# Two transformer blocks in one kernel: the same tiles at other places in the on-chip memory

## What is computed

```python
h = h + conformer_conv(h, ...)
h = h + swiglu_ffn(h, ...)
kv = shared_kv(h, ...)
h = h + nsa_attention(h, ..., kv)
h = h + swiglu_ffn(h, ...)
x = rmsnorm(h, final_norm)
for layer in range(2):
    h = rms_norm(x, g_mix[layer])
    x = x + (even_mixer(h, ...) if layer == 0 else odd_mixer(h, ...))
    x = x + memory_cross_attention(rms_norm(x, g_xa[layer]), m, ...)
    x = x + swiglu(rms_norm(x, g_ffn[layer]), ...)
```

## Time and profile before

| what | value |
|---|---|
| median of 3 runs | 2776.31 us (2769.07 to 2776.97) |
| the profiled execution | 2776.31 us, of which the span of its instructions is 2774.5 us |
| mean granted TensorE clock | 0.965 |
| TensorE busy with products | 2632.7 us, 95% of the span |
| VectorE, ScalarE, GpSimd busy | 51%, 34%, 13% |
| DMA | 219.83 MB, 79 GB/s over the span |

### The profile page before, as it was taken

How to read it: one execution, slowest core, us unless ns; L and a number is a source line. 1 busy time by engine, 2 the same in 40 slices (tenths; PEclk the granted TensorE clock), 3 DMA queues, 4 the chain that set the end, 5 groups by cost and what they waited for, 6 DMA issues and landing times.

```text
span 2774.5 us, 34029 instructions
## 1 busy us (share of the span) xinstructions
PE 2632.7 (95%) x12132; PEld 2150.2 (77%) x12132; DVE 1403.0 (51%) x2125; ACT 942.1 (34%) x1645; POOL 350.1 (13%) x312
## 2 busy tenths in 40 slices
PE   6988999999889999999989898999999999899999
PEld 5866888887777788888768686788887877688887
DVE  5885544335577544434443565544433656544422
ACT  4554332222366333322333434323222124332321
POOL 2002000110055400012100040200011050200000
PEclk9999999999699999999998999999999999999999
DMA  4202333233100133323321022233323322133232
GB/s 147 74 1 61 101 96 97 76 108 120 64 1 1 46 99 93 96 76 106 100 84 31 16 82 71 76 97 93 92 84 103 98 90 91 42 102 95 91 101 69
DMA packets 61006, 219.83 MB, mean 79 GB/s; under 512 B 7136, under 2 KB 7392, under 8 KB 60400
## 3 DMA queue, kind: packets, MB, share of 16 engines
q1 hardware_dynamic: 58896, 209.15, 24.2%
q0 software_dynamic: 2016, 9.44, 1.0%
HBM read 216.47 MB, written 2.10 MB: 79 GB/s over the span
## 4 chain that ended last, share of the span: by engine, by line
PE 87%; DVE 8%; ACT 2%; issue 2%; POOL 0%; DMA 0%; DVEq 0%; ACTq 0%; SPq 0%; POOLq 0%
PE psum L212 25%; PE psum L213 25%; PE psum L214 24%; DVE conv_out L847 2%; PE psum L1796 2%; PE psum L1774 1%; DVE wl L195 1%; PE psum L1158 1%; PE psum L1210 1%; ACT wh L189 1%; PE psum L1756 1%; PE psum L1757 1%; PE psum L2581 1%; PE psum L1977 1%; DVE xl L748 1%
## 5 line engine op out<-in xcount | busy, mean ns | idle before, releaser
L212 PE MATMUL psum<-xh,wh 128*128 128x512 f32 x1880 | 744.7, 396 | 51.8 <-DVE xl L748 25.4
L213 PE MATMUL psum<-xl,wh 128*128 128x512 f32 x1880 | 740.0, 394 | 0.0
L214 PE MATMUL psum<-xh,wl 128*128 128x512 f32 x1880 | 739.1, 393 | 0.0
L189 ACT ACTIVATE wh<-raw 128x1024 fp32r<-128x1024 f32 x404 | 421.0, 1055 | 790.2 <-PE psum L214 790.2
L195 DVE TENSOR_TENSOR wl<-raw,wh 128x1024 fp32r<-128x1024 f32 x404 | 532.2, 1330 | 262.5 <-ACT wh L189 261.7
L212 PEld LDWEIGHTS psum<-xh,wh 128*128 128x128 f32 x1880 | 357.0, 190 | 132.5 <-DVE xl L748 31.0
L214 PEld LDWEIGHTS psum<-xh,wl 128*128 128x128 f32 x1880 | 356.9, 190 | 77.0 <-issue 1.5
L213 PEld LDWEIGHTS psum<-xl,wh 128*128 128x128 f32 x1880 | 356.9, 190 | 74.8 <-issue 1.2
L212 PE MATMUL psum<-hidden_high,wh 128*128 128x512 f32 x704 | 276.0, 392 | 0.0
L213 PE MATMUL psum<-hidden_low,wh 128*128 128x512 f32 x704 | 274.1, 389 | 0.0
L214 PE MATMUL psum<-hidden_high,wl 128*128 128x512 f32 x704 | 274.0, 389 | 0.0
(11 more groups left out here) (381 smaller groups left out, 3354.8 us busy)
## 6 DMA issues: line engine op xcount, KB each, us to landing
raw<-ffn_in SPq DMA_DIRECT2D x176, 512.0 KB, 3.5
raw<-ffn_out SPq DMA_DIRECT2D x64, 448.0 KB, 4.1
raw<-ffn_out SPq DMA_DIRECT2D x32, 512.0 KB, 3.6
raw<-pw SPq DMA_DIRECT2D x24, 512.0 KB, 3.6
raw<-o_w_hgg SPq DMA_DIRECT2D x12, 512.0 KB, 4.2
raw<-w_q SPq DMA_DIRECT2D x8, 512.0 KB, 3.6
raw<-w_o SPq DMA_DIRECT2D x8, 512.0 KB, 3.5
raw<-e_w_qk SPq DMA_DIRECT2D x8, 512.0 KB, 3.6
```

The source lines that it names most:

```text
L189: self.nc.scalar.activation(self.wh[:, slot, :], self.raw[:, slot, :], ACT.Copy).then_inc(self.weights_high.sem, 1)
L212: nc.tensor.matmul(out, ah, bh, start=start, stop=False)
L213: nc.tensor.matmul(out, ah, bl, start=False, stop=False)
L214: return nc.tensor.matmul(out, al, bh, start=False, stop=stop)
```

## The change

The order in which `Core.__init__` places its tiles is another one. Sizes, arena offsets, stages, instructions, waits and their order stay as they are.

```diff
-        self.wh = self.place("wh", [P, SLOTS, PANEL], FR)
-        self.wl = self.place("wl", [P, SLOTS, PANEL], FR)
+        self.x = self.place("x", [P, KD, S])
         self.xh_at = self.at
         self.xh = self.place("xh", [P, KD, S], FR)
         self.xl_at = self.at
         self.xl = self.place("xl", [P, KD, S], FR)
-        self.arena0 = self.at
-        self.at += ARENA * 1024
-        self.x = self.place("x", [P, KD, S])
         self.raw = self.place("raw", [P, SLOTS, PANEL])
+        self.wh = self.place("wh", [P, SLOTS, PANEL], FR)
+        self.wl = self.place("wl", [P, SLOTS, PANEL], FR)
         self.rstd = self.place("rstd", [P, S])
...
-        self.ssq_at = self.at
         self.ssq = self.place("ssq", [P, S])
...
         self.eps = self.place("eps", [P, 1])
+        self.arena0 = self.at
+        self.at += ARENA * 1024
         self.psum = ctx.enter_context(nc.psum_tensor("psum", [P, 8, S], F32))
```

## The result

| | before | after |
|---|---|---|
| median, us | 2774.06 (2769.07 to 2777.38, 6 runs) | 2795.11 (2792.77 to 2796.22, 6 runs) |
| ratio, 95% interval | | 1.0077 (1.0063 to 1.009) |
| profiled execution, its span | 2776.31, 2774.5 | 2795.92, 2794.1 |
| mean granted TensorE clock | 0.965 | 0.965 |
| instructions | 34029 | 34029 |

The forecast was 2776 us (2768 to 2782), no change. The kernel is slower by 0.77%, which is where the second rival lay (2792 to 2798).

A forecast was written before the change was run, and what follows sets the result against it. TensorE, busy 95% of the span and 87% of the chain, was taken as the bound. With no instruction changed, every address term was put at 0 us, summing to 0 on the profiled 2776.31: 2776 us, range 2768 to 2782.

The forecast's parts named there:

- the second rival: Arena trains in feed-forward second products and six attention and mixer outputs don't settle: 16 to 22 us slower, 2792 to 2798; chance 0.21.
- Nothing for instructions, order and waits: All queues: no instruction removed, added or moved, no wait goes by an address, loop starts cost the same; 0 us.
- Moves by multiples of 256, 0 us: Tiles outside the arena move by multiples of 256 bytes; the region leaves no mark on the products' pitch; 0 us.
- The arena's new rest on products, 0 us: Large products streaming arena tiles, start at rest 32 in place of 128: constant relation, so trains settle at 226.7 ns again; 0 us.
- a rule by lines of 16 bytes: Skill's rule for SBUF reads: accesses within a 16-byte line run at full rate, so a multiple of 32 is as good as 64.
- The bound of 16.3 to 21.5 us if it doesn't settle: 3264 arena-streaming products at 5.0 ns more each (pitch of `Gates`) or 6.6 ns more (taps' 233.3).
- Nothing hides it: TensorE is the bound where the arena's products run, so a slower pitch there would show in full, 16.3 to 21.5 us.
- The count of 3264: Large products that stream an arena tile: 3 x 704 for `hidden` and 3 x 64 for each of six tiles.
- GpSimd, 0 us: Arena work in the cross-attentions, 8 pairs per layer: taken as 0, with 6 us kept as an end; as a rival, chance 0.05.
- DMA, 0 us: `raw` keeps its rest, SyncE's queue is idle nearly always, loads into the arena come early and are few; 0 us.
- VectorE, 0 us: VectorE's taps read rows at all multiples of 4, median 740 ns, against 744 on even rows; 0 us.

The follow-up runs named there:

- the steps of 32: Kernel of trains alone: weight start moves on 32 bytes from product to product, moving operand with it, eight constant differences; 230.8 to 234.2 ns a product.
- the alternating trains: Kernel of trains alone: products alternate between two pairs of weight and moving starts, own or next weights in step; 232.1 and 230.4 ns with 32, 228.5 and 230.0 with 128.
- the constant trains: Kernel of trains alone, 48 products each at one fixed difference of moving and weight start: 226.7 ns at 0, 229.2 at 64, 233.3 at 32, 234.2 at 160.

## Why the prediction was wrong

- *Nothing for instructions, order and waits*: right. The count is 34029 in both, and the kernel with the same new order and the arena at a rest of 128 takes the time before.
- *Moves by multiples of 256, 0 us*: right, and shown: 928 products of `xh` in the same 210 us, and a ratio of 1.0005 with all other tiles in new places.
- *The arena's new rest on products, 0 us*: this is the step that failed, in the sentence "My reading is that such a train settles at 226.7 again". It took the 226.7 of the earlier trace rows as the pitch of any train with a constant relation, when it was the pitch of one relation, difference 0, which all settled trains of the kernel before happened to have. A train does settle, but at a pitch of its own: 234.2 at 160, 233.1 to 233.5 at most others, 229.2 at 64. The right reading was within reach of the rows: the earlier trace rows had other relations and other pitches, and I put that down to change from product to product. The runs show that a change of start at a constant difference costs as well (230.8 to 234.2 in the steps of 32), so both belonged in the sum. A premise ahead of this step failed with it, that the start matters on a scale of 16 bytes on which every multiple of 32 is even: a shift of 16, 32 or 128 is as little free as one of 4 (231.7, 233.3, 233.3 and 236.7 ns). So a rule by lines of 16 bytes, which leaves the sum at nothing, doesn't hold for these products.
- *The bound of 16.3 to 21.5 us if it doesn't settle*: 24.5 us by the products' own pitch, because 160 is dearer than the taps' mean; 19.6 of them in the span and 21 between the medians. "Nothing hides it" was wrong as well: shorter waits for `wl` and `xl` and the clock gave some of it back. The count of 3264 leaves out 96 products that stream `wh` or `wl` over arena weights (233.5 ns after, some 0.6 us more) and 192 with 256 columns (281 ns in place of 283, some 0.4 us less).
- *GpSimd, 0 us*: right. `mem_sq` has a median of 614 ns in both. *DMA, 0 us*: right, a panel still lands after 3.5 us and the chain has none of it. *VectorE, 0 us*: its shifted taps went from a median of 740 to 748 ns (1.1 us over 142, in front of the wait for `conv_out`); medians of 743 to 757 stand in the other kernels here, and the one that changes `OURS` alone, with every tile at its old place, has 744, so no rule can be read from it.
- The second rival was right in place, sign and time. Its words for the mechanism (a train that never settles) were not, and 0.21 was too little for it: of the constant relations a new start can have in steps of 32, one in eight costs nothing. That its range held the time is in part luck: its price came from trains that are slow for other reasons and was too low, and nothing was taken off for what is given back.

What stays open is the mechanism below the difference: which reads meet which. Neither the own weights alone nor the next ones alone explain the alternating trains, and what the two cost together does not add up from the constant trains.

## What to carry to other kernels

When tiles are moved, keep the start of each moving operand equal to that of its weights modulo 256, and the same from product to product, where the products are 128 by 128 by 512 in the rounded 32-bit format, or measure one train of 48 at the new starts: it takes 11 us, and its pitches here were those of the whole kernel. A small tile placed ahead of a large region shifts everything in that region; here one of 4 bytes that takes 32 cost 0.77%. And when every row of a profile shares a property, the profile can't say what that property is worth: count it as an open term, not as zero.

## What the runs showed of the hardware that was not expected

- The pitch of a large rounded 32-bit product depends on the difference of two start addresses: 226.7 ns at 0 modulo 256, 229.2 at 64, 233.1 to 234.2 at the other multiples of 32 (moving operand shifted); bfloat16 (215.8) and plain 32-bit records (429.1) don't show it.
- At 256 columns difference 0 is not the best: 120.2 ns against 117.9 at 32.
- Starts 4 and 16 past a multiple of 32 cost even at difference 0: 237.7 and 231.0 ns.
- Part of what slower products take can come back behind them: a wait of 2.38 us became 1.13, the granted clock there 0.82 and 1.00, and the stretch of 18.7 us became 14.5.
